# First input chunk of a convolution multiplied tile by tile between the transposes before it

## The reference, cut to what matters

```python
h = modulate(rms_norm(x, norm1_g[layer]), sh1, sc1)
u = h @ w_in + b_in                         # 1024 -> 2048
u = u[..., :D] * jax.nn.sigmoid(u[..., D:]) # values * sigmoid(gates)
u = depthwise causal convolution of u, 31 taps, + b_dw
u = jax.nn.silu(layer_norm(u, ln_g, ln_b))
x = x + g1 * (u @ w_out + b_out)
```

## Time and profile before

| | us |
|---|---|
| median of 3 runs (2066.47 to 2070.1) | 2068.57 |
| the profiled execution's own time | 2066.58 |
| its span, first to last instruction | 2064.8 |
| TensorE busy | 1904.0 (92%) |
| VectorE busy | 1182.1 (57%) |
| ScalarE busy | 483.3 (23%) |

### The profile page before, as it was taken

One profiled execution on the slowest core, in us unless ns is written; L12 is line 12 of the kernel. 1 busy time (PEld: TensorE's weight loads), 2 busy tenths in 40 slices (PEclk: granted clock), 3 DMA queues, 4 the chain that ended last, 5 costly groups with the idle time before them and its releaser, 6 DMA issues.

```text
span 2064.8 us, 49936 instructions
## 1 busy us (share of the span) xinstructions
PE 1904.0 (92%) x19736; PEld 1182.4 (57%) x19736; DVE 1182.1 (57%) x2101; ACT 483.3 (23%) x1017; POOL 303.1 (15%) x464
## 2 busy tenths in 40 slices
PE   6999999999999959999999489999899699999990
PEld 3444444445666636777777367655444477777770
DVE  4548500478899953333333569999995433333336
ACT  3110100456777730000000230000535000000002
POOL 0001120000000012222222400000001122222223
PEclk9999999799999979999999689999999799999995
DMA  9557520100530089768985703043106899954456
GB/s 395 222 204 290 199 62 0 42 11 24 199 125 6 16 337 369 258 253 295 370 333 206 292 1 108 2 122 107 52 0 243 306 408 407 336 202 173 174 174 259
DMA packets 122780, 391.43 MB, mean 190 GB/s; under 512 B 23841, under 2 KB 44961, under 8 KB 118433
## 3 DMA queue, kind: packets, MB, share of 16 engines
q1 hardware_dynamic: 72720, 303.48, 38.7%
q0 software_dynamic: 21904, 66.99, 9.0%
q10 hardware_dynamic: 28032, 19.17, 3.1%
HBM read 337.33 MB, written 47.49 MB: 186 GB/s over the span
## 4 chain that ended last, share of the span: by engine, by line
PE 85%; DVE 8%; DMA 4%; ACT 1%; issue 1%; SPq 0%; POOL 0%; ACTq 0%; DVEq 0%; POOLq 0%
PE ps L1668 24%; PE ps L1678 12%; PE ps L1720 10%; PE ps L1494 9%; PE ps L1605 5%; PE ps L1549 5%; PE ps L1563 4%; PE ps L1576 4%; PE ps L1588 4%; DVE kv L1376 3%; PE ps L1792 3%; DMA kv<-in_w_ada 2%; PE ps L1757 1%; DVE pbuf L1060 1%; DMA kv<-in_w_gate_up 1%
## 5 line engine op out<-in xcount | busy, mean ns | idle before, releaser
L1668 PE MATMUL ps<-kv,hT 128*32 128x256 f32 x5504 | 386.8, 379 | 1.3 <-DMA kv<-in_w_gate_up 1.3
L1668 PEld LDWEIGHTS ps<-kv,hT 128*32 128x32 f32 x5504 | 240.9, 110 | 63.3 <-issue 1.9
L1376 DVE SCALAR_TENSOR_TENSOR kv<-kv,cols 128x640 f32<-128x640 f32 (+1 forms) x330 | 266.2, 807 | 11.2
L1249 DVE TENSOR_TENSOR hT<-hT,modc 128x256 f32<-128x256 f32 x146 | 62.1, 425 | 332.7 <-PE ps L1668 332.6
L1720 PE MATMUL ps<-hT,ring 128*128 128x320 f32 (+1 forms) x768 | 225.9, 455 | 6.3 <-ACT hT L673 6.3
L1494 PE MATMUL ps<-hT,ring 128*128 128x512 f32 x512 | 223.3, 597 | 1.2 <-DVE hT L1040 1.2
L788 ACT ACTIVATE hT<-ps 128x128 f32<-128x128 f32 x146 | 40.5, 277 | 741.6 <-PE ps L1668 741.6
L1073 DVE TENSOR_TENSOR_SCAN pbuf<-hT 128x128 f32<-128x128 f32 (+7 forms) x128 | 173.1, 1353 | 47.0 <-ACT hT L730 46.7
L1720 PEld LDWEIGHTS ps<-hT,ring 128*128 128x128 f32 x768 | 146.5, 192 | 82.3 <-ACT hT L673 6.9
L1494 PEld LDWEIGHTS ps<-hT,ring 128*128 128x128 f32 x512 | 97.2, 191 | 125.2 <-issue 123.3
L1668 PE MATMUL ps<-ring,hT 128*32 128x256 f32 x2560 | 151.0, 387 | 13.0 <-DVE hT L1249 11.4
(11 more groups left out here) (254 smaller groups left out, 2387.5 us busy)
## 6 DMA issues: line engine op xcount, KB each, us to landing
kv<-in_w_gate_up SPq DMA_DIRECT2D x136, 512.0 KB
kv<-in_w_ada SPq DMA_DIRECT2D x20, 2048.0 KB, 7.8
ring<-in_w_gate_up SPq DMA_DIRECT2D x80, 512.0 KB
kv<-in_w_down SPq DMA_DIRECT2D x48, 512.0 KB
ring<-in_w_down SPq DMA_DIRECT2D x40, 512.0 KB
hT<-in_w_gate_up SPq DMA_DIRECT2D x40, 512.0 KB
expert_rows<-hT ACTq DMA_DIRECT2D x584, 32.0 KB
ring<-in_w_in SPq DMA_DIRECT2D x32, 512.0 KB, 12.1
```

The source lines that it names most:

```text
L1376: ins = V.scalar_tensor_tensor(new, old, w_dw_c[:, c, k:k + 1], new, ALU.mult, ALU.add)
L1668: ins = mm(bank(0)[UNIT * q:UNIT * (q + 1), 0:2 * P], xT[:, c, :], wset[s][q // 2][:, 512 * c + 256 * (q % 2):512 * c + 256 * (q % 2) + 25 ...
```

## The change

TensorE's order becomes: turn tiles 0 and 1; then for t = 0 to 4 the part of chunk 0's gates and values that belongs to tile t (`first_input(t, 0)`, `first_input(t, 1)`, 16 instructions of 128 columns each), with turn(t + 1) or, for the last, tile 5's turn between gates and values; then the gates of step 1, turn(6), the values of step 1, turn(7), the gates and values of step 2, and the wait for tile 7's eviction. So chunk 0's 64 instructions of 320 columns become 160 of 128 columns. In PSUM, tiles 0 to 2 lie in the first bank of a pair and tiles 3 and 4 in the second, so `gate(0)` and `gated(0)` become two instructions each, of 384 and 256 columns. ScalarE takes `gate(0)` after evicting tile 5, and `gate(1)` after tile 6. VectorE evicts tiles 6 and 7 ahead of taps 7 and 17 of its first half-chunk. Tile 5's turn goes to bank 0.

```diff
+KEPT_AT = {(0, 7): FIRST + 1, (0, 17): FIRST + 2}
...
-            return (2, 4, 2, 4, 2, 0, 2, 0)[t] if n == 3 else (0, 2, 0, 2, 4, 2, 4, 2)[t] if n == 0 else 0 if t == TT - 1 else 2 * (t % 2)
+            return (2, 4, 2, 4, 2, 0, 2, 0)[t] if n == 3 else (0, 2, 0, 2, 4, 2, 4, 2)[t] if n == 0 else 0 if t >= FIRST else 2 * (t % 2)
...
+        def first_column(t):
+            return P * t if t < 3 else 512 + P * (t - 3)
+
+        FIRST_PARTS = ((0, 3), (3, FIRST))
...
+                if i == 0:
+                    for t0, t1 in FIRST_PARTS:
+                        at = 512 * gates_bank(0) + first_column(t0)
+                        ins = nc.scalar.activation(usig[:, 0, P * t0:P * t1], ps[:, at:at + P * (t1 - t0)], ACT.Sigmoid,
+                                                   bias=b_in_c[:, 8:9])
+                    ins.then_inc(usig_done, 1)
+                    return
...
-                if t == FIRST + 1:
+                if t == FIRST + 2:
                     gate(0)
+                if t == FIRST + 3:
+                    gate(1)
...
-            act.wait_ge(h_turned, 3 * TT)
-            for i in range(1, 2 * DC):
+            for i in range(2, 2 * DC):
                 gate(i)
...
-                if t >= 2:
+                if 2 <= t < FIRST + 3:
                     norm_keep(2, t - 2)
...
+                if i == 0:
+                    for t0, t1 in FIRST_PARTS:
+                        src = 512 * values_bank(0) + first_column(t0)
+                        ins = V.scalar_tensor_tensor(u_all[:, 0, at + P * t0:at + P * t1], ps[:, src:src + P * (t1 - t0)],
+                                                     b_in_c[:, 0:1], usig[:, 0, P * t0:P * t1], ALU.add, ALU.mult)
+                    ins.then_inc(u_done, 1)
+                    return
...
                 for k in range(CW):
+                    if (d, k) in KEPT_AT:
+                        norm_keep(2, KEPT_AT[d, k])
...
+            def first_input(t, part):
+                pe.wait_ge(cv_loaded[part], 16 * PARTS)
+                turned(2, t)
+                to = ps[:, 512 * (gates_bank, values_bank)[part](0):][:, first_column(t):first_column(t) + P]
+                for k in range(DC):
+                    ins = mm(to, ring[:, part, 512 * k:512 * k + P], hT[:, k, t * P:(t + 1) * P],
+                             start=(k == 0), stop=(k == DC - 1), skip_group_check=True)
+                if t == FIRST - 1:
+                    ins.then_inc((gates_done, values_done)[part], 1)
...
+            turn(2, 0)
+            for t in range(FIRST):
+                if t < FIRST - 1:
+                    turn(2, t + 1)
+                first_input(t, 0)
+                if t == FIRST - 1:
+                    turn(2, FIRST)
+                first_input(t, 1)
+            gated_input(1, 0)
             turn(2, FIRST + 1)
...
             for i in range(1, 2 * DC):
                 if i >= 2:
                     pe.wait_ge(u_done, i - 1)
-                gated_input(i, 0)
+                    gated_input(i, 0)
                 pe.wait_ge(usig_done, i)
                 gated_input(i, 1)
+                if i == 1:
+                    turn(2, TT - 1)
+                if i == 2:
+                    turned(2, TT - 1)
```

More of the change, by code:

```diff
@@ L1706, in _ @@
             moe(0)
-            for t in range(FIRST):
-                turn(2, t)
-            turned(2, FIRST - 1)
+            def first_input(t, part):
[7 more added lines that the diff above has]
+                    ins.then_inc((gates_done, values_done)[part], 1)
             def gated_input(i, part):
@@ L1794, in project_out @@
                 ins.then_inc(out_done, 1)
-            gated_input(0, 0)
-            turn(2, FIRST)
+            turn(2, 0)
[7 more added lines that the diff above has]
+            gated_input(1, 0)
             turn(2, FIRST + 1)
-            gated_input(0, 1)
-            turn(2, FIRST + 2)
-            turned(2, TT - 1)
             for i in range(1, 2 * DC):
```

## The result

| | before | after |
|---|---|---|
| median, us | 2068.6 (2066.47 to 2070.1, 4 runs) | 2051.95 (2049.01 to 2053.57, 4 runs) |
| profiled execution, us | 2066.58 | 2052.51 |
| its span, us | 2064.8 | 2050.7 |

The ratio is 0.9919, 95% interval 0.9901 to 0.9936: 16.7 us faster where 15.2 were forecast, and 2051.95 us where 2053.4 were. The interval is 13 to 20 us of gain, so the timed runs can't tell 15.2 from 16.7; how well the terms of the sum fit is read from the traces.

A forecast was written before the change was run, and what follows sets the result against it. Bounds: VectorE from its first `gated` on, TensorE close behind. Earlier `gated(0)` 17.2, longer `gated(0)` -0.1, first tap +0.95, wait -0.35, two evictions -2.54: 15.2 us, so 2068.57 - 15.2 = 2053.4 us, range 2050 to 2058.

The forecast's parts named there:

- The diagnosis: VectorE from its first `gated` on and TensorE close behind both bound the stage; to gain, both have to begin earlier.
- The price of the short instructions: TensorE's 160 new 128-column instructions: 0.111 us each at full clock, 0.23 at half, if load and matmul overlap.
- rivals 2 and 3: Short matmuls hide weight loads partly (0.165 us, 2062.0 us, chance 0.12) or not at all (0.22 us, 2070.8 us, 0.07).
- Rival 4: TensorE's clock stays at 1.2 GHz through the tile-wise part of chunk 0; slower, 2076.8 us, chance 0.07.
- First `gated`: VectorE's start of `gated(0)`, at 1201.15 instead of 1218.33: 17.2 us gained.
- the stated bound of 15.6: Gain in us if TensorE cost nothing, since ScalarE's root 7 holds from 1196.9.
- ScalarE's table load: 1.28 us after ScalarE's eviction of tile 5, before hidden in a wait, now on the path to `gated(0)`.
- First tap: VectorE's first tap takes 0.65 us instead of 1.57, as GpSimd builds its taps sooner: another 0.95 us gained.
- Wait at tap 7: VectorE waits for turn(6)'s result ahead of evicting tile 6: 0.35 us lost.
- Two evictions: VectorE's evictions of tiles 6 and 7, moved between taps, 1.27 us each: 2.54 us lost.
- Nothing after 1522 depends on absolute time: Behind the taps, from 1522 us in the trace, work only shifts, so the end moves by as much.
- TensorE stays ahead of VectorE: TensorE leads by 17.4 us, more than VectorE's gain, so it stays ahead of every later `gated`.

The follow-up runs named there:

- e1: The changed kernel, but VectorE evicts tiles 6 and 7 ahead of its first gated operation again; 2067.37 us, ratio to before 0.9998.
- e2: The changed kernel, but chunk 0's gates and values made whole as before, 320 columns at a time after tile 4 is kept; 2066.95 us, ratio to before 0.9995.
- e10: The changed kernel without GpSimd's four later preparations of taps, a small memset in their place, part of the convolution not computed; one run, 2052.25 us.
- e3: The changed kernel with the values of each tile of chunk 0 made twice, 80 more instructions of 128 columns; 2059.78 us, ratio to before 0.9955.
- e5: The changed kernel, but ScalarE evicts all 8 chunks of tiles 6 and 7 and VectorE none; 2050.2 us, ratio to before 0.9908.
- e7: The changed kernel with 14 extra products of 512 columns on TensorE ahead of the turn of tile 0; one run, 2051.87 us.
- e8: The changed kernel with GpSimd's first preparation of taps held back until VectorE's first gated operation is done; one run, 2052.51 us.
- e9: On top of e5, ScalarE also evicts all of tile 5 behind its first gate, VectorE folds earlier, statistics and scales two taps later; 2049.51 us, ratio to before 0.9908.
- e11: As e7, but with 19 extra products ahead of the turn of tile 0 and one more behind it; one run, 2052.55 us.

## Why the prediction was right

**The diagnosis** that a VectorE busy for 57% of the span is one of two bounds of this stage held. In e1 TensorE's chunk 0 was as early as in after and only VectorE's start late, and the whole gain was lost; in e2 VectorE's start was held back by TensorE's whole chunk 0, with the same result. That TensorE is the other bound, close behind, is shown by e10: VectorE was relieved of 5.0 us and the end moved by 1.1.

**The price of the short instructions**, the term that divided forecast from rivals 2 and 3, was 0.1116 us against my 0.111. It had come from rows of other forms, with a single pair at half clock the only one of the same form; that this was enough was partly luck. The Trainium skill ("TensorE: Matmul & The Clock Gate", Back-to-back issue gap) gives 81 ns for a load and a 128-column matmul in a stream where the bare matmul has 56, an estimated 0.16 us here. This trace doesn't agree for float32 on 128x128 weights: the 128 instructions of tiles 1 to 4 keep 0.1116 us. Rival 4 fell as well: the clock rose at 1178.9 in the time of before's trace, where I had 1180. I had it 6.9 us after turn(1) began; in after and in e1, e3, e5, e7, e8, e9 and e10 it rose 4.7 to 5.9 us after it.

**The sum by its terms**, in time behind the first combine. First `gated`: 17.2 us earlier forecast, 17.76 measured; the clock rose a little sooner, so turn(5) ended 0.6 sooner, and from there on ScalarE's root 7 held, as the stated bound of 15.6 has it. ScalarE's table load did lie on the path, 1.28 us of it. Longer first `gated`: 0.1, and 0.15 measured. First tap: 0.95 gained, and 0.96 measured (1.57 to 0.61 us). Wait at tap 7: 0.35 and 0.35. Two evictions: 2.54 and 2.57. That makes 15.2 forecast and 15.70 measured at `gated(1)`.

**What the sum left out** came behind it: the end of the taps moved by 16.97, 1.27 us more than `gated(1)`. The taps' busy time fell from 266.2 to 265.0 us with not one tap changed. e8 and e10 show why: GpSimd's four later operations each lengthen a tap, and by how much depends on where in a tap they fall; behind the first combine they came 18.2 us earlier, as TensorE triggers them, and `gated(1)` only 15.7, so each met another moment of another tap. I had taken everything after `gated(1)` as shifted by a constant. That was wrong by 1.3 us, in favour here by luck; e5 got 1.1 us of it the other way. In e2, forecast at 2069.4 and measured at 2066.95, the taps ended 1.1 us before those of before instead of 0.8 after them, and 1.3 of these 1.9 us came behind `gated(1)` in the same way. "Nothing after 1522 depends on absolute time" held within 0.4 us between these two traces (543.24 us from the end of the taps to the end of the span, and 542.80), but over all traces this rest is 542.8 to 545.7 us, so part of every single time is not the change's.

**TensorE stays ahead of VectorE**: right, with no wait for values; its step 2 began 18.1 us earlier where 17.4 were forecast. I had named no number for how much of this lead would be left; e10 gives about 1 us at the statistics, and that is what a next step would run into.

## What to carry to other kernels

Where two engines run a stage side by side, read each one's first and last instruction of the stage and not its share of the span: here moving one start alone brought nothing, and the gain was the smaller of the two shifts (15.7 and 18.1 us). A price for a stream that isn't in the trace can be put together from a weight-bound row, a transpose row and one pair of the right form, if both ends of the bracket are carried to the final time. And compare traces from a common event inside the program: 3.3 us of drift in the first layer would otherwise have hidden terms of 0.4 us. Know the scatter that is left, too: 0.5 us here between the first and the last combine, so that terms of this size are safe only within one trace.

## What the runs showed of the hardware

- A tap of 640 columns with two tensors in SBUF that meets a GpSimd operation of 1024 columns took up to 2.42 us in after (2.51 in before) instead of 0.89; the 640-column `gated` of before, with one tensor in PSUM, took 0.87 beside the same operation. The first tap, with one tensor in SBUF and none in PSUM, took 1.57 us beside it and 0.61 alone. GpSimd's own operation took 1.91 us where it met no running tap and up to 2.59 (e7) where it began beside one. The Trainium skill ("SBUF — State Buffer", Who interferes with whom) says that a VectorE instruction with two SBUF inputs and a GpSimd instruction that reads SBUF contend for one interface and that the first to start blocks the other. The traces agree for the taps with two tensors in SBUF, with 5.0 us over four operations.
- TensorE's clock: after the added products of e7 it went from 1.00 to 0.50 within the 5.25 us without work ahead of turn(0), and was down from 1169 on. In e11 the idle times before the turns were 1.36 and 1.43 us, and it stayed at 1.00; in e1 it was at 0.50 behind an idle time of 2.79 us.
- Load and matmul overlap in the short stream too: at 1.00 an instruction of 128 columns takes 0.1116 us, one of 320 columns 0.27. Per column that is nearly the same (0.87 and 0.84 ns), but one of 1 column took 0.113 us; so whether the columns or the weight load set the 0.1116 us isn't shown.
